# Block compression reads its moving operand from a turned tile that VectorE writes, instead of from the pages

## The reference

```
def nsa_compress(kb, w1, b1, w2):
    hid = jax.nn.gelu(jnp.einsum('bnphd,pde->bnhe', kb, w1) + b1)
    return hid @ w2
```

## Time and profile before

| | |
|---|---|
| median of 3 runs | 4248.86 us (4248.82 to 4249.32) |
| span of the profiled execution, first to last instruction | 4247.0 us |
| mean granted clock of TensorE over the span | 0.929 |
| PE busy in the span | 3621.8 us, 85% |
| DVE busy in the span | 1500.9 us, 35% |
| `compress`, first PE record at L948 to the end of the last DVE copy | 1571.6 to 1834.4 us |

### The profile page before, as it was taken

The page is one execution under the profiler, slowest core; times in us unless marked ns, Lnnn a source line. Parts: engine busy times, 40 slices in busy tenths (PEclk is TensorE's granted clock), DMA queues, the critical chain, the costliest instruction groups (busy, mean ns, idle before and its releaser), DMA issues. The chain is left out here.

```text
span 4247.0 us, 65977 instructions
## 1 busy us (share of the span) xinstructions
PE 3621.8 (85%) x24514; PEld 3322.3 (78%) x24514; DVE 1500.9 (35%) x3250; ACT 1081.8 (25%) x2124; POOL 374.9 (9%) x507
## 2 busy tenths in 40 slices
PE   4999999948999539968888877999788399999995
PEld 3999999938999539956665655777688299999994
DVE  5333333270111010024444445555631623232335
ACT  2212121121111010014433345444422321212122
POOL 1000000021000011013232300000000300000001
PEclk7999999978999869979998979999899699999997
DMA  2111111004433363248887711000053111111111
GB/s 78 40 49 40 49 40 46 28 0 133 121 92 92 138 209 119 89 159 312 303 303 287 283 56 40 6 6 6 20 157 114 30 40 41 44 44 44 40 44 42
DMA packets 293885, 401.78 MB, mean 95 GB/s; under 512 B 50197, under 2 KB 222614, under 8 KB 293638
## 3 DMA queue, kind: packets, MB, share of 16 engines
q1 hardware_dynamic: 255654, 309.55, 22.6%
q0 software_dynamic: 24368, 79.26, 5.3%
q10 hardware_dynamic: 13680, 10.72, 0.8%
HBM read 356.17 MB, written 47.27 MB: 95 GB/s over the span
## 5 line engine op out<-in xcount | busy, mean ns | idle before, releaser
L423 PE MATMUL ps<-f_hh,f_wh 128*128 128x364 f32 x2112 | 697.0, 330 | 81.7 <-DVE f_wl L368 81.7
L423 PE MATMUL ps<-f_hl,f_wh 128*128 128x364 f32 x2112 | 696.9, 330 | 0.0
L423 PE MATMUL ps<-f_hh,f_wl 128*128 128x364 f32 x2112 | 696.5, 330 | 0.0
L423 PEld LDWEIGHTS ps<-f_hh,f_wh 128*128 128x128 f32 x2112 | 398.4, 189 | 83.0 <-issue 83.0
L423 PEld LDWEIGHTS ps<-f_hl,f_wh 128*128 128x128 f32 x2112 | 399.0, 189 | 0.0
L423 PEld LDWEIGHTS ps<-f_hh,f_wl 128*128 128x128 f32 x2112 | 398.9, 189 | 0.0
L573 PE MATMUL ps<-pj_hh,pj_wh 128*128 128x364 f32 (+1 forms) x936 | 309.0, 330 | 52.3 <-DVE pj_wl L558 52.3
L443 PE MATMUL ps<-f_uh,f_wl 128*128 128x364 f32 x1056 | 348.6, 330 | 0.0
L443 PE MATMUL ps<-f_ul,f_wh 128*128 128x364 f32 x1056 | 346.6, 328 | 0.0
L443 PE MATMUL ps<-f_uh,f_wh 128*128 128x364 f32 x1056 | 345.9, 328 | 0.0
L368 DVE TENSOR_TENSOR f_wl<-f_raw,f_wh 128x1024 fp32r<-128x1024 f32 x132 | 157.2, 1220 | 506.0 <-ACT f_wh L342 484.6
(11 more groups left out here) (360 smaller groups left out, 5620.3 us busy)
## 6 DMA issues: line engine op xcount, KB each, us to landing
dpage<-cache_diff_kv SPq DMA_DIRECT2D x256, 512.0 KB, 7.4
f_raw<-ffn_w SPq DMA_DIRECT2D x132, 512.0 KB, 4.2
npage<-cache_nsa_kv POOLq DMA_DIRECT2D x256, 128.0 KB, 5.7
z_scratch<-pj_z POOLq DMA_DIRECT2D x38, 546.0 KB
pj_raw<-w_in SPq DMA_DIRECT2D x38, 512.0 KB, 4.2
pages<-cache_nsa_kv SPq DMA_DIRECT2D x96, 128.0 KB, 4.2
pages<-cache_nsa_kv POOLq DMA_DIRECT2D x80, 128.0 KB, 5.5
pages<-cache_nsa_kv ACTq DMA_DIRECT2D x80, 128.0 KB, 5.2
```

The lines of the kernel that those rows point to most:

```text
L423: last = pe.matmul(G.ps[:, s + c, 0:CH], w[a][:, j % 3, k * P:(k + 1) * P], h[b][:, k, c * CH:(c + 1) * CH], start=(k == 0 and n == 0), st ...
```

## The change

DVE gets a part in the main work of `compress`. A new tile `turned` has two slots, each for 16 of the 64 dimensions of one kind of a chunk: 16 x 48 x 2 numbers in a partition, with the dimension outermost. For each chunk DVE makes eight copies (`turn_pages`: 2 kinds x 4 parts), each from `pages` into a slot, and raises `slot_filled`. PE waits for the slot, multiplies the 16 dimensions of it, now with 96 columns that lie side by side, and raises `slot_used`; DVE waits for that before it fills the slot again. The place of a chunk in `pages` is free when DVE has copied it (`slot_filled`), no longer when PE has multiplied it. The waits for the loaded pages move from PE to DVE. The activation waits for `slot_used` in place of `hid_ready` and `multiplied`. DVE's copies of the projected blocks of round g - 1 now stand between its two chunks of round g. The loops over rounds, `Fori` before, are written out in full.

```diff
+        DIMS = 16
+        parts = HD // DIMS
+        turned = sb("turned", [P, 2, DIMS, chunk, KVH])
...
+        slot_filled, slot_used = sem("slot_filled"), sem("slot_used")
...
         def load(eng, which, g, c, s):
             eng.wait_ge(cleared, 2)
-            eng.wait_ge(multiplied[c], g)
+            if g > 0:
+                eng.wait_ge(slot_filled, ((g - 1) * 2 + c + 1) * 2 * parts)
             load_pages(nc, G, eng, which, g, c, s)
...
-            def hidden(g, c, last=False):
-                for s in range(3):
-                    pe.wait_ge(page_in[c][s], g * (16 * share) + (16 * share, 0, 16)[s if last else 0])
+            def hidden(g, c):
                 for kind in range(2):
-                    pe.wait_ge(hid_done[kind], g * 2 + c)
-                    for d in range(HD):
-                        mm = pe.matmul(G.ps[:, kind, 0:chunk * KVH], w1[:, kind, d, :], pages[:, c, :, kind, :, d],
-                                       start=(d == 0), stop=(d == HD - 1))
-                        if d == HD - 1 and kind == 0:
-                            mm.then_inc(hid_ready, 1)
-                mm.then_inc(multiplied[c], 1)
+                    if g * 2 + c > 0:
+                        pe.wait_ge(hid_done[kind], g * 2 + c)
+                    for part in range(parts):
+                        n = kind * parts + part
+                        pe.wait_ge(slot_filled, (g * 2 + c) * (2 * parts) + n + 1)
+                        for i in range(DIMS):
+                            d = part * DIMS + i
+                            mm = pe.matmul(G.ps[:, kind, 0:chunk * KVH], w1[:, kind, d, :], turned[:, n % 2, i, :, :].rearrange("p a h -> p (a h)"),
+                                           start=(d == 0), stop=(d == HD - 1))
+                        mm.then_inc(slot_used, 1)
...
                 for kind in range(2):
-                    ready, count = ((hid_ready, g * 2 + c + 1), (multiplied[c], g + 1))[kind]
                     act.wait_ge(weights_in, 16 * 8)
-                    act.wait_ge(ready, count)
-                    act.wait_ge(c_ready, g)
+                    act.wait_ge(slot_used, (g * 2 + c) * (2 * parts) + (kind + 1) * parts)
+                    if g > 0:
+                        act.wait_ge(c_ready, g)
...
+            def turn_pages(g, c, last=False):
+
+                for s in range(3):
+                    dve.wait_ge(page_in[c][s], g * (16 * share) + (16 * share, 0, 16)[s if last else 0])
+                for kind in range(2):
+                    for part in range(parts):
+                        n = kind * parts + part
+                        before = (g * 2 + c) * (2 * parts) + n
+                        if before >= 2:
+                            dve.wait_ge(slot_used, before - 1)
+                        dve.tensor_copy(turned[:, n % 2, :, :, :],
+                                                 pages[:, c, :, kind, :, part * DIMS:(part + 1) * DIMS].rearrange("p a h d -> p d a h")).then_inc(slot_filled, 1)
...
+            for g in range(rounds):
+                turn_pages(g, 0)
+                if g > 0:
+                    keep_blocks(g - 1)
+                turn_pages(g, 1, g == rounds - 1)
+            keep_blocks(rounds - 1)
```

More of the change, by code:

```diff
@@ L903, in compress @@
         hid = sb("hid", [P, 2, npages, KVH])
+        DIMS = 16
+        parts = HD // DIMS
+        turned = sb("turned", [P, 2, DIMS, chunk, KVH])
         sem = sem_maker(nc, ctx, "cp")
         cleared, weights_in = sem("cleared"), sem("weights_in")
-        hid_ready, hid_done = sem("hid_ready"), [sem(f"hid_done{kind}") for kind in range(2)]
-        multiplied = [sem(f"multiplied{c}") for c in range(2)]
+        hid_done = [sem(f"hid_done{kind}") for kind in range(2)]
+        slot_filled, slot_used = sem("slot_filled"), sem("slot_used")
         c_ready, c_copied = sem("c_ready"), sem("c_copied")
@@ L923, in _ @@
             load(pool, mybir.EngineType.Pool, 0, 1, 2)
-            with pool.Fori(1, rounds - 1) as g:
+            for g in range(1, rounds - 1):
                 for c in range(2):
@@ L927, in _ @@
             load(pool, mybir.EngineType.Pool, rounds - 1, 0, 2)
-            pool.wait_ge(multiplied[1], rounds - 1)
+            pool.wait_ge(slot_filled, (rounds - 1) * 4 * parts)
             pool.dma_start(pages[:, 1, share:share + TILES, :, :, :].rearrange("t a k h d -> t a (k h d)"),
@@ L935, in _ @@
             load(sp, mybir.EngineType.SP, 0, 1, 0)
-            with sp.Fori(1, rounds) as g:
+            for g in range(1, rounds):
                 for c in range(2):
@@ L941, in _ @@
         def _(pe):
-            def hidden(g, c, last=False):
-                for s in range(3):
-                    pe.wait_ge(page_in[c][s], g * (16 * share) + (16 * share, 0, 16)[s if last else 0])
+            def hidden(g, c):
                 for kind in range(2):
-                    pe.wait_ge(hid_done[kind], g * 2 + c)
-                    for d in range(HD):
-                        mm = pe.matmul(G.ps[:, kind, 0:chunk * KVH], w1[:, kind, d, :], pages[:, c, :, kind, :, d],
-                                       start=(d == 0), stop=(d == HD - 1))
-                        if d == HD - 1 and kind == 0:
-                            mm.then_inc(hid_ready, 1)
-                mm.then_inc(multiplied[c], 1)
+                    if g * 2 + c > 0:
[8 more added lines that the diff above has]
+                        mm.then_inc(slot_used, 1)
             def project_blocks(g):
                 pe.wait_ge(hid_done[0], g * 2 + 2)
-                pe.wait_ge(c_copied, g)
+                if g > 0:
+                    pe.wait_ge(c_copied, g)
                 for half in range(2):
@@ L969, in _ @@
             pe.wait_ge(weights_in, 16 * 8)
-            with pe.Fori(0, rounds - 1) as g:
+            for g in range(rounds - 1):
                 hidden(g, 0)
@@ L974, in _ @@
             hidden(rounds - 1, 0)
-            hidden(rounds - 1, 1, last=True)
+            hidden(rounds - 1, 1)
             project_blocks(rounds - 1)
@@ L1000, in _ @@
             load(act, mybir.EngineType.Activation, 0, 1, 1)
-            with act.Fori(0, rounds - 2) as g:
+            for g in range(rounds - 2):
                 for c in range(2):
@@ L1012, in _, with keep_blocks @@
         def _(dve):
-            with dve.Fori(0, rounds) as g:
+            def turn_pages(g, c, last=False):
[9 more added lines that the diff above has]
+                                                 pages[:, c, :, kind, :, part * DIMS:(part + 1) * DIMS].rearrange("p a h d -> p d a h")).then_inc(slot_filled, 1)
+            def keep_blocks(g):
                 dve.wait_ge(c_ready, g + 1)
```

## The result

The changed kernel takes 4174.9 us (median of 4 runs, 4168.6 to 4178.8) against 4249.1 us; the ratio is 0.9814, with a 95% interval of 0.9803 to 0.9826. That is 79 us less (74 to 84), 1.9% faster; 4166 us were forecast. The profiled execution took 4168.6 us with a span of 4167.1 us. Runs of one kernel spread by some 10 us here, before and after, so in what follows the length of the stage in the trace is compared, from PE's first record to the end of DVE's last copy. It repeats within 1 us: 140.0 and 139.6 us in e10_quarter_arrays and e12_quarter_timed, which are one kernel.

The account below looks back on a forecast made before the run. PE, busy throughout `compress` and slowed by the step of its moving columns, was taken as the bound. 4248.86 us less 83.1 saved on PE, with copies, handovers and loads hidden, gave 4166 us, between 4161 and 4181.

Parts of the forecast that it names:

- The pace before and after: PE's records in `compress`: 166.2 ns apart before, because of the columns' step; 111.4 ns with dense columns, set by weight load.
- The cold records: PE's first 20 records, at granted clock 0.50, start 222 ns apart whatever the columns and gain nothing.
- The copies: DVE's 48 copies into `turned`: 1.75 us each, bounds 0.95 and 3.1, hidden by PE's work on the other slot.
- The cover: PE's 3.57 us on the other slot hides a copy with handovers, 2.27 us; without it the copies cost 109 us.
- My count of the handovers: Between PE and DVE at each slot: 0.18 us plus 0.34 us, added to every copy.
- The loads: Page loads by SP, POOL and ACT come 2 to 7 us early, though a chunk to hide behind shrinks to 28.5 us.
- The rival in which POOL is starved: DVE's copies hold off POOL's page loads, which come 10 to 11 us late three times: 4200 us; chance 0.12.
- The written-out loops: Writing out the loops over rounds costs nothing: the last round, already written out, took 85.29 us against 85.28.
- The rival with the sign turned: DVE becomes the bound from 4.8 us a copy on and the kernel is slower, 4335 us at 6.6; chance 0.08.

Follow-up runs that it names:

- e10_quarter_arrays: The change, but each matmul made as two of 64 x 64, leaving out the weight matrix's two zero quarters; 4143.6 us in one run.
- e12_quarter_timed: The same kernel as e10_quarter_arrays (the change with 64 x 64 matmul pairs), timed again in rounds; 0.9714 of the kernel before, 4135.3 us.
- e8_five_chunks: The change, but the 264 pages in five chunks (104 or 112 columns) instead of six, slots of 8 dimensions; 0.9764 of the kernel before, 4149.9 us.
- e9_half_columns: The change, but each first-layer matmul takes only 48 of the 96 columns; 4330.0 us in one run, the kernel before beside it 4251.2.
- e5_twice: The change, but every copy into `turned` made twice, with a wait between; 0.9818 of the kernel before.
- e6_thrice: The change, but every copy into `turned` made three times, with waits between; 4218.3 us in one run.
- e7_two_inputs: The change, but the copy made by a two-input operation, the larger of the part and itself; 0.9848 of the kernel before, 4188.9 us.
- e4_straight: The change without its tile and copies: PE reads and frees the pages itself, loops still written out; 0.9993 of the kernel before.

## Why the prediction was right, step by step

**The pace before and after** was right: 166.2 ns came from the step, and 111.4 ns for dense columns was measured as (57.41 - 0.278) / 511 = 111.8 ns. The reading that the rest is the weight load held: more columns change nothing (e8_five_chunks at full clock, e9_half_columns at half), smaller weights do (e10_quarter_arrays).

**The cold records** gain nothing, as said. Their 222 ns were read too high, since the length of a warm record was taken off a cold stream: with 456 ns, the longest at L1493, it is (4.94 - 0.456) / 21 = 213.5 ns, as in e9_half_columns. So there were 1.11 / (0.2134 - 0.1662), some 24, before and not 20. After, the first round is 60.26 - 57.41 = 2.85 us longer than the second, at 213.4 - 111.8 ns each some 28. With these paces and counts PE saves 24 x 213.4 + 1512 x 166.2 - 28 x 213.4 - 1508 x 111.8 ns = 81.8 us. The saving in the stage was 81.9 us where 83.1 were forecast. The profiled execution shows it nearly whole; the interval of the timed ratio, 74 to 84 us, holds it.

**The copies** took 1.50 us; 1.75 was taken, with bounds of 0.95 and 3.1. The cover held even at twice the work. My count of the handovers was wrong in kind: the second slot hides them when the copy is clearly shorter than PE's slot (e5_twice) or clearly longer (e6_thrice), and part of them shows only when the two are nearly equal (e7_two_inputs). So by estimate the point at which DVE would make the kernel slower lies at 42.6 / 8 = 5.3 us a copy, not at 4.8.

**The loads** came in time, with POOL's burst 1.6 us longer. ACT, which was the latest, as forecast, had issued its 16 at 1606.26 + 12.45 = 1618.7; a median landing of 4.6 us makes it 1623.3, and the copy that reads these pages began at 1628.51, behind a wait for PE. So they were some 5 us early, within the forecast's 2 to 7; by the longest landing, 8.5 us, it is 1.3. The rival in which POOL is starved had its mechanism right and its price wrong: the copies do hold POOL off (e7_two_inputs), but DVE waits 2.07 us of every 3.57, and in that time POOL catches up; only with DVE nearly always busy does an issue typically take 1.4 us.

**The written-out loops** at nothing: shown by e4_straight.

**The rival with the sign turned** (a copy over 4.8 us) did not happen. e7_two_inputs came nearest: the strided read costs a two-input operation 3.67 us, more than my upper bound of 3.1 for the copy. No row of the kernel before reads SBUF on DVE at such a step, so that the copy came out below the 1.75 taken was in part luck. Had it cost as much as in e7, the cover would have gone, and 9.6 us of the stage with it.

## What to carry to other kernels

Compare the pace of a stream of matmuls with that of another stream of the same shape in the same trace, and with one of fewer columns: the first shows whether the operand's layout costs, the second whether the columns set the pace or something else does. A transposing copy on an idle engine costs nothing when it is shorter than the matmuls on one slot; with two slots the handovers count only where the two are nearly equal. When the weight load is the floor, more columns to a load or splitting off the zero quarters of the weights can pay: here 28.5 and 41 us of the stage.

## What the runs showed of the hardware that was not expected

- With 48 moving columns TensorE ran 335 us without a pause at a granted clock of 0.50, in one run (e9_half_columns); with 96 and the same weight loads the clock was 1.00 some 6 us after the start (the change).
- At a step of 16 bytes a record takes 173.5 ns, more than at 64 bytes (164.9) or in the pages (166.2).
- Two 64 x 64 matmuls on opposite quarters take 82.5 ns together, one of 128 x 128 with the same columns 111.8.
- A two-input operation on VectorE that reads 1536 numbers at the pages' steps of 256 and 768 bytes takes 3.67 us, the one-input copy 1.50, and 0.96 in runs of 16 numbers.
